# Wanted rows of V summed on TensorE, lists and shares some blocks earlier, and 80 instead of 72 blocks of U ahead of V

## The reference, cut to what matters

```python
scores = einsum('thpc,hpnc->thpn', q, sub_keys)        # 8 heads, 2 halves, 128 keys each
top_s, top_i = top_k(scores, 16)                        # per half
best_s, best_pos = top_k(all 16 x 16 sums of a head, 16)
idx  = key number of half 0 * 128 + key number of half 1     # one of 16384 experts
gate = softmax(best_s)                                  # 8 x 16 = 128 experts a token
act  = gelu(x . expert_u[idx])                          # exact gelu
y    = sum over the 128 experts of gate * act * expert_v[idx]
h    = layer_norm(alpha * h + y)
```

## Time and profile before

| | us |
|---|---|
| median of 3 runs | 2716.87 (2714.51 to 2718.97) |
| profiled execution, its own time | 2720.42 |
| its span, first to last instruction | 2718.6 |
| PE busy | 2324.0 (85%) |
| DVE busy | 1563.2 (57%) |
| ACT busy | 630.0 (23%) |
| POOL busy | 587.8 (22%) |

### The profile page before, as it was taken

How to read it: one execution, slowest core, us unless ns; L and a number is a source line. 1 busy time by engine, 2 the same in 40 slices (tenths; PEclk the granted TensorE clock), 3 DMA queues, 4 the chain that set the end, 5 groups by cost and what they waited for, 6 DMA issues and landing times. The chain is left out here.

```text
span 2718.6 us, 42249 instructions
## 1 busy us (share of the span) xinstructions
PE 2324.0 (85%) x16604; PEld 1702.5 (63%) x16604; DVE 1563.2 (57%) x3014; ACT 630.0 (23%) x1540; POOL 587.8 (22%) x625
## 2 busy tenths in 40 slices
PE   8989988999998689987978888768998798888874
PEld 8978865555553387887854545338788785545541
DVE  5787543110000154488996666675448799666666
ACT  4543322000000045222311111114522131111111
POOL 0011200111111100001224554530000121544553
PEclk9999988999999899999999999989999898999997
DMA  7420026999999671389999999977138899999996
GB/s 226 144 68 3 3 109 250 414 419 419 419 419 420 276 273 32 119 316 345 350 367 410 404 408 411 395 267 260 32 130 314 316 337 360 409 408 410 408 401 269
DMA packets 223236, 797.64 MB, mean 293 GB/s; under 512 B 37238, under 2 KB 103286, under 8 KB 165312
## 3 DMA queue, kind: packets, MB, share of 16 engines
q1 hardware_dynamic: 150224, 450.15, 43.2%
q0 software_dynamic: 72816, 344.80, 32.3%
HBM read 881.07 MB, written 11.27 MB: 328 GB/s over the span
## 5 line engine op out<-in xcount | busy, mean ns | idle before, releaser
L2462 PE MATMUL psum<-v_raw,act 128*128 128x512 f32 x1024 | 509.1, 630 | 163.9 <-DMA v_raw<-expert_v_dram,all_gates 158.2
L2436 PEld LDWEIGHTS psum<-all_gates 128*128 128x128 f32 x4096 | 503.4, 200 | 127.5 <-issue 82.5
L2436 PE MATMUL psum<-all_gates 128*128 128x128 f32 x4096 | 512.9, 284 | 60.7 <-DMA all_gates<-expert_u_dram 39.2
L2569 POOL DMA_INDIRECT all_gates<-expert_pairs_dram,all_gates x256 | 261.1, 1020 | 1192.0 <-DVE all_gates L2706 532.2
L2462 PEld LDWEIGHTS psum<-v_raw,act 128*128 128x128 f32 x1024 | 183.8, 196 | 403.5 <-DMA v_raw<-expert_v_dram,all_gates 246.4
L2606 DVE CUSTOM_DVE_ANT_0 all_gates<-all_gates,psum 128x1024 f32<-128x1024 f32 x204 | 249.1, 1221 | 283.8 <-DMA all_gates<-expert_pairs_dram,all_gates 283.6
L2617 DVE SCALAR_TENSOR_TENSOR psum<-all_gates,psum 128x1024 f32<-128x1024 f32 x254 | 326.4, 1285 | 12.3 <-ACT all_gates L2530 12.0
L1741 PE MATMUL psum<-piece_raw,tile_cols 128*64 128x256 f32 x2496 | 290.8, 384 | 17.8 <-DMA piece_raw<-w_up_dram 7.7
L1741 PEld LDWEIGHTS psum<-piece_raw,tile_cols 128*64 128x64 f32 x2496 | 177.9, 138 | 131.0 <-issue 38.0
L2528 ACT ACTIVATE all_gates<-all_gates 128x1 f32<-128x1 f32 x256 | 51.7, 202 | 811.3 <-DVE all_gates L2606 811.3
L2578 POOL DMA_INDIRECT v_raw<-expert_v_dram,all_gates x224 | 222.0, 991 | 74.1 <-issue 67.3
(11 more groups left out here) (527 smaller groups left out, 3433.0 us busy)
## 6 DMA issues: line engine op xcount, KB each, us to landing
all_gates<-expert_u_dram SPq DMA_DIRECT2D x256, 512.0 KB, 7.6
piece_raw<-w_gate_dram SPq DMA_DIRECT2D x78, 1024.0 KB, 18.7
piece_raw<-w_up_dram SPq DMA_DIRECT2D x78, 1024.0 KB, 19.6
piece_raw<-w_down_dram SPq DMA_DIRECT2D x78, 1024.0 KB, 21.2
in_raw<-w_in_dram SPq DMA_DIRECT2D x48, 1024.0 KB, 5.3
query_raw<-w_query_dram SPq DMA_DIRECT2D x16, 1024.0 KB, 6.1
v_raw<-expert_v_dram SPq DMA_DIRECT2D x32, 512.0 KB, 10.2
w_o<-w_o_dram SPq DMA_DIRECT2D x16, 512.0 KB
```

What stands on the lines that cost most here:

```text
L2436: last = nc.tensor.matmul(PS[:, bank, 0:P], raw_u[:, n % RAW_U, c * P:(c + 1) * P], h_full[:, c, :], start=(c == 0), stop=(c == KD - 1), s ...
L2462: last = nc.tensor.matmul(PS[:, 4 + m, :], slot(n), raw_v[:, n % RAW_V, m * BANK:(m + 1) * BANK], start=(n == 0), stop=(n == N - 1), skip_ ...
L2569: nc.gpsimd.indirect_dma_start(out=ring[:, r, :, :].rearrange("p h d -> p (h d)"), out_offset=None, in_=S["pair_rows"], in_offset=bass.Ind ...
```

## The change

In each layer:

- `sum_gates` is new. After all 16 spreads PE sums `G` over the tokens with 32 matmuls: the identity in bfloat16 is the stationary operand, the upper 16 bits of the float32 gates (read as bfloat16, two elements apart) the moving one, 4 tokens (512 columns) a matmul, all added in PSUM bank 0. DVE's `want` is one piece of work now: it waits for the sums, adds the 4 parts, and makes all 128 columns of the load list at once.
- V blocks are loaded whole only up to block 9 (`WHOLE` = 10) instead of 15.
- The dense choice's shares come 2 to 4 blocks earlier on ACT, its exponential 2, the lists 4 (after 46 blocks).
- `E` is 80 instead of 72: PE scores 34 blocks of U beside the 16 spreads instead of 22, and 48 instead of 56 beside V. The 8 more slots of `act` lie in the upper half of the `all_gates` buffer.

```diff
@@
 EARLY = 72
+MORE = 8
@@
-    N, E, PICKS = NKEYS, EARLY, PH * TOPK
+    N, E, PICKS = NKEYS, EARLY + MORE, PH * TOPK
-    EXP_AFTER = (14, 43)
-    LISTS_AFTER = 50
+    EXP_AFTER = (14, 41)
+    LISTS_AFTER = 46
-    SHARES_AFTER = (26, 28, 32, 35, 37, 39, 42, 44, 46, 48)
+    SHARES_AFTER = (24, 26, 30, 33, 34, 36, 39, 41, 43, 44)
-    WHOLE, PARTS = 16, 4
+    WHOLE = RAW_V + 3
@@
+        upper_half = G.bitcast(BF16).rearrange("p t (j o) -> p t j o", o=2)[:, :, :, 1]
+        sums = PS[:, 0, :].rearrange("p (t j) -> p t j", j=P)
@@ TensorE
+                def sum_gates():
+                    pe.wait_ge(ident_known, 1)
+                    pe.wait_ge(g_out, SPREAD)
+                    for t in range(0, P, 4):
+                        last = nc.tensor.matmul(sums, ident_half, upper_half[:, t:t + 4, :], start=(t == 0), stop=(t == P - 4))
+                    last.then_inc(summed, 1)
@@
+                sum_gates()
                 pe.wait_ge(acted, E)
                 for n in range(N):
                     back(n)
                     for m in dense_after(n):
+                        if m == E:
+                            pe.wait_ge(wanted_known, 1)
                         dense(m)
@@ GpSimd
-                    part = (n - WHOLE) * PARTS // (N - WHOLE)
-                    pool.wait_ge(wanted_known, part + 1)
+                    pool.wait_ge(wanted_known, 1)
@@ VectorE
-                def want(part):
-                    size = (N - WHOLE) // PARTS
-                    j = slice(WHOLE + part * size, WHOLE + (part + 1) * size)
-                    step(nc.vector.tensor_reduce(wanted[:, j], G[:, :, j].rearrange("p t j -> p j t"), X, ALU.max))
+                def want():
+                    dve.wait_ge(summed, 1)
+                    step(nc.vector.tensor_reduce(wanted, sums.rearrange("p t j -> p j t"), X, ALU.add))
...
-                    if n in (0, 1, 2, 3):
-                        want(n)
+                    if n == 0:
+                        want()
```

More of the change, by code:

```diff
@@ L2302, in small_experts @@
     LAST_BLOCKS = 2
-    WHOLE, PARTS = 16, 4
+    WHOLE = RAW_V + 3
     with phase(nc, "dve_step x_turned h_full_done scores_done scores_out exp_ready exp_done rows_done lists_t lists_out "
-                   "hot_done g_done g_out picks_known dotted gelu_done shared x_copied own_known wanted_known") as (
+                   "hot_done g_done g_out picks_known dotted gelu_done shared x_copied own_known wanted_known ident_known summed") as (
             memory, dve_step, x_turned, h_full_done, scores_done, scores_out, exp_ready, exp_done, rows_done, lists_t,
-            lists_out, hot_done, g_done, g_out, picks_known, dotted, gelu_done, shared, x_copied, own_known, wanted_known), \
+            lists_out, hot_done, g_done, g_out, picks_known, dotted, gelu_done, shared, x_copied, own_known, wanted_known, ident_known, summed), \
         phase(nc, "u_in0 u_in1 u_in2 u_in3 v_in0 v_in1 v_in2 v_in3 v_in4 v_in5 v_in6 row_in0 row_in1 row_in2 row_in3 "
@@ L2318, in small_experts @@
         stats = sbuf(nc, memory, "ln_stats2", [P, NT, 16])
+        ident_half = sbuf(nc, memory, "ident_half", [P, P], BF16)[:, :]
         sbuf(nc, memory, "peer_arena", [P, arena_bytes // 4])
@@ L2323, in at @@
             return nc.alloc_sbuf_tensor_at(f"{name}_{nc.next_id()}", shape, F32, offset=base + kb * KB)
-        act = at("act", 0, [P, E, P])
+        act = at("act", 0, [P, EARLY, P])
+        more_act = S["all_gates"][:, P:P + MORE, :]
         raw_v = at("v_raw", 36, [P, RAW_V, D])
@@ L2367, in slot @@
         def slot(n):
-            return act[:, n % E, :]
+            return act[:, n % E, :] if n % E < EARLY else more_act[:, n % E - EARLY, :]
         def picks_after(n):
@@ L2743, in gate @@
                     tt(slot(n), slot(n), G[:, :, n], ALU.mult).then_inc(gated, 1)
-                def want(part):
-                    size = (N - WHOLE) // PARTS
-                    j = slice(WHOLE + part * size, WHOLE + (part + 1) * size)
-                    step(nc.vector.tensor_reduce(wanted[:, j], G[:, :, j].rearrange("p t j -> p j t"), X, ALU.max))
-                    step(ts(wanted[:, j], wanted[:, j], 0.0, float(1 << 20), ALU.is_le, ALU.mult))
-                    step(tt(wanted[:, j], wanted[:, j], block_row[:, j], ALU.add))
-                    nc.vector.tensor_copy(load_row[:, j], wanted[:, j]).then_inc(wanted_known, 1)
+                def want():
+                    dve.wait_ge(summed, 1)
+                    step(nc.vector.tensor_reduce(wanted, sums.rearrange("p t j -> p j t"), X, ALU.add))
+                    step(ts(wanted, wanted, 0.0, float(1 << 20), ALU.is_le, ALU.mult))
+                    step(tt(wanted, wanted, block_row, ALU.add))
+                    nc.vector.tensor_copy(load_row, wanted).then_inc(wanted_known, 1)
+                nc.vector.tensor_copy(ident_half, C["ident"]).then_inc(ident_known, 1)
                 step(tt(wanted, C["ident"], C["iota"], ALU.mult))
```

## The result

The changed kernel takes 2699.2 us (median of 4 runs, 2696.1 to 2701.7) against 2717.9 for the kernel before (4 runs, 2714.5 to 2719.4): ratio 0.993, 95% interval 0.991 to 0.995. On another chip, with more runs of both, the ratio was 0.9947 (0.9928 to 0.9967). It is 18.7 us faster where 27 were forecast; the time lies in the stated range.

The account below looks back on a forecast made before the run. DMA bytes at 408 GB/s bound the V stage, DVE the spread stage. Layer 1: +5.3 - 17.0 = -11.7; layer 2: +1.8 - 17.0 = -15.2; together -26.9 us, from median 2716.9 to 2690; range 2674 to 2711.

Parts of the forecast that it names:

- eight blocks: V stage: taking 8 U blocks out of a stage bound by bytes at 408 GB/s saves 10.3 us a layer.
- Rival (c): V stage follows its rings, not bytes, so removing U blocks gives nothing: +20.6 us, 2711; chance 0.07.
- Lists: End of the choice: PE's lists come 7.5 us earlier in layer 1, 11 in layer 2; bounds 3 and 12.
- Rival (e): Lists don't come earlier because DVE is late, 3 us instead: +12, 2702; chance 0.20 together with rival (a).
- The spread stage: PE becomes the bound with 50 pieces, 89.5 us against DVE's 79.7 (+9.8), plus 3 us of stalls a layer.
- rival (a): Spread stage stalls at the choice's pace, PE waiting for U at 1.2 GHz: 98 us, +11, 2701; 0.20 with (e).
- DMA at or above 370 GB/s in the stage: Sign that the forecast is right: DMA's rate in the spread stage is at least 370 GB/s.
- waits for U of more than 8 us: Sign that the forecast is wrong: PE waits for U blocks more than 8 us in a spread stage.
- The sums: After the spreads: PE's 32 one-pass matmuls of 512 columns take 0.24 us each, 7.6 us in all.
- (b): The sums' 4-byte pitch halves PE's rate: sums 15.2 us, +15 in all, 2705; chance 0.07.
- (d): The sums cost as float32 work: 28.8 us on PE, +42 in all, 2732; chance 0.06.
- The V stage's beginning: Loss of DMA time there falls to 3 us from 6.8 and 7.3: -4 us a layer; bounds -7 and 0.

Follow-up runs that it names:

- e4: The changed kernel with E = 72 instead of 80 (no more U blocks ahead of V): 2686.0 us, ratio 0.987 to the kernel before.
- e1: The kernel before with only the dense choice's shares, exponential and lists moved earlier (lists after 46 blocks): 2700.1 us, ratio 0.9916 to the kernel before.
- e2: The kernel before with only the sums on PE, want in one piece and V whole up to block 9: 2702.5 us, ratio 0.9932.
- e3: The kernel before with only E = 80 instead of 72 blocks of U ahead of V: 2719.4 us, ratio 1.0002.
- e9: The changed kernel (E = 80) with 5 instead of 4 buffers for U: 2678.4 us, ratio 0.985 to the kernel before.
- e5: The changed kernel unchanged, run again as reference on another chip: 2698.7 us, ratio 0.9947 to the kernel before.
- e8: The changed kernel with 16 V blocks loaded whole instead of 10: 2702.7 us, ratio 0.9953 to the kernel before.
- e6: The changed kernel with E = 76 instead of 80: 2693.3 us, ratio 0.9909 to the kernel before.

## Why the prediction was right, and where not

**What bounds.** Right. The V stage moved by bytes: eight blocks fewer made it 9.6 and 10.7 us shorter (changed against e4), where 10.3 stood. Rival (c) falls.

**Lists.** Taken as 7.5 and 11; by the profiles 7.5 and 18.6, by e1 5.9 and 17, 22.8 us in all by its ratio. DVE was ready at 1266.8 (1266.5 forecast) and PE's block 45 was the later, as said. Layer 2's 131.0 of before was high for an unchanged choice: e2 had 124.6, e3 128.1. The mean of the six unchanged ones in the table is 126.6, of the eighteen with earlier lists and four buffers 114.8: 11.8 a layer, where 9.3 was taken on the mean. Rival (e) falls.

**The spread stage: the step that failed.** The prediction took PE's 89.5 us and 3 of stalls, 12.8 over DVE's 79.7. From the first spread to the sums the changed kernel takes 94.9 and 98.2, 15.2 and 18.5 over 79.7, so 5.4 and 8.7 of stalls; the eight such stages with 50 pieces and four buffers take 94.9 to 99.0, 96.5 on the mean, 7.0 of stalls. The 3 us were the term that was mis-sized; 8.6 was the upper bound.

Two things make them up. First, PE starts the stage at the lower of its two clocks (1.2 GHz) after 4.67 us without work: the first spread and the two blocks after it take 3.22 and 4.24 us in layer 1, 3.78 and 4.82 in layer 2, where later ones take 1.95 and 3.74. That is 1.8 and 2.9 us, which no rival had, and which DVE's longer time had hidden before. Second, PE waits for U, 3.0 and 3.8 us; the wait of 3.03 in layer 2 is followed by a block of 3.62 us instead of 1.95, 1.7 more. This second part is what rival (a) describes, a wait and then the lower clock; layer 2 reaches rival (a)'s length (98), but only 5.5 of its 8.7 us come from there. The granted clocks of 0.98 and 0.95 agree: 1.9 and 4.9 us lost.

That the kernel before had no waits for U in the stage was taken as a sign against rival (a), but there PE had slack between its pieces. e9 takes the waits away and the stage is 90.8 and 91.2; it is the test that shows this part. The rule of the Trainium skill (TensorE: Matmul & The Clock Gate, HAM oscillation — how this bites in real kernels), that waits for DMA put TensorE back to its half clock, is borne out by that one block; rival (a), with (e), had 0.20 and deserved more. Of the signs named beforehand, DMA at or above 370 GB/s in the stage failed (361 and 352), and waits for U of more than 8 us did not come.

The prediction's own terms had the eight blocks at a loss of 2.5 us a layer (12.8 against 10.3), and did not say so: that part of the change was summed under others with which it does not belong. e4 and e5 put the loss at 13 us or more for both layers.

**The sums.** 32 matmuls in 7.2 us, 0.225 each (0.24 taken), the rate of one pass. The 4-byte pitch cost nothing against the 0.118 us of 256 columns, as the Trainium skill has it (SBUF — State Buffer, Door 1: The DMA port swizzle). Rivals (b) and (d) fall. The same section of the Trainium skill says that PSUM accesses which are not contiguous slow down matmuls. A reduction of DVE shows no such cost: it reads PSUM at a pitch of 512 bytes and took 0.69 us (0.9 taken), 1.35 ns an element against 1.74 for the maxima from SBUF. The V stage's beginning: 407 - 378 GB/s over 51.2 us is 3.6 us lost, and 1.0 in the sums; 3 was taken, for 6.8 before. In layer 2 it is 3.5 and 2.0. So 4.6 and 5.5 us are lost where 3 was taken.

**The sum.** By milestones of the profiles, layer 1: lists -7.5, from there to the first `back` +22.3 (7.2 of it the sums), V -24.5: -9.7 (forecast -11.7). Layer 2: -18.6 + 25.2 - 20.9 = -14.3 (forecast -15.2). With -0.9 ahead of layer 1, -0.3 between the layers and +0.9 behind them this is -24.3. The medians give -18.7. The 5.6 between them is within the scatter of single runs (2708 to 2726 for the kernel before over 23 runs on one chip), larger than the 3.5 us by which the prediction set its profile apart.

That the time came within 10 us of the forecast is in part luck: on the mean of the profiles the lists gave some 5 us more than forecast over both layers and the spread stage cost 8 us more, and the two errors stand against each other. The upper end of the range, 2711, is rival (c) alone; with (a), (b) and (c) together, as it is put there, it would be 2737.

Not settled: why V in layer 2 shrank by 20.9 only, whether the six V blocks by rows give their 2.7 us a layer (e8: 4.1 us in both by medians, 1.6 by ratios, of 5.4), why 46 pieces took 93 us in e6 and 86.5 in e3, and whether the span of 114 helps.

## What to carry to other kernels

When work is moved from a stage bound by one resource into the slack of another, price it at the point where the slack ends: here a block cost next to nothing up to the level of PE and DVE, then 1.7 to 1.8 us for 1.28 gained, and more with waits. Sum each part of a change by itself before adding: two good parts (0.9916 and 0.9932) carried one that took a third or more of their gain away. And when an engine becomes the bound, its buffers must be deep enough for the new rhythm: one more buffer of 0.5 MB was worth 20 us or a little more.

## What was not expected of the hardware

The fifth buffer: landing times of U's blocks in layer 1's spread stage were 4.7 to 9.9 us (median 7.8) with five and 4.2 to 9.9 (median 6.9) with four, so what the buffer bought is not a faster landing but more lead. An estimate from the pieces: a load may start when the block four before is scored, and between that and its own turn PE has three blocks and two spreads, 5 * 1.79 = 8.95 us, less than the longest landing; with five buffers it has four blocks and two or three spreads, 10.7 us or more. The sums were as fast as forecast, and worth knowing all the same: one 512-column matmul on 16-bit values read two elements apart runs at 0.225 us, a quarter of the 0.90 us of its float32 neighbour, so a sum over 16384 gates a row costs 7.2 us on TensorE where a maximum took VectorE 25.
